# Index products of two heads side by side, with the first pair of a chunk issued inside the logits

## The chip, the cores and the metric

The kernel runs on one core of one Trainium2 chip. The core has five engines that run on their own and meet at semaphores: TensorE (PE, with PEld for its weight loads), VectorE (DVE), ScalarE (ACT), GpSimd (POOL) and SyncE (SP, which here only issues DMAs). The metric is the device time of one execution in microseconds (us).

## What is computed

One decoder layer over 2048 tokens of width 1024, in float32: layer norm, one projection, a pooling mixer and an attention over selected keys, the output projection, a second norm, and a mixture of 32 experts of which each token uses four. The change lies in the attention. There an indexer with 8 heads of width 64 scores every key for every query, and the 256 best keys are kept:

```python
s = jnp.einsum('bqhd,bsd->bqhs', iqb, ikf)                       # 8 index heads, width 64
idx_score = jnp.einsum('bqhs,bqh->bqs', jax.nn.relu(s), iwb * w_scale)
idx_score = jnp.where(causal, idx_score, NEG_INF)
_, sel = lax.top_k(idx_score, 256)
logits = jnp.einsum('bqgrd,bqkgd->bqgrk', qg, k_sel) * (HEAD_DIM ** -0.5)
```

## The kernel before

The program has stages one behind the other: projection (up to about 574 us), attention (574 to about 2290 us), a short placement of tokens to experts, the experts (to about 5100 us), and the combination. The attention stage (`attend_stage`) goes over 16 blocks of 128 queries. Block b sees 128(b+1) keys, `keys[b]`. The keys are cut into chunks of `BANK` = 512, one PSUM bank; the last chunk can be 128, 256 or 384 wide. Blocks 0 and 1 need no selection, so there are scores for blocks 2 to 15 only, 38 chunks in all, 28 of them 512 wide.

The order of the work is written out by hand in `walk`, which every engine runs through with functions of its own. For each of the 6 attention heads of block b it calls `logits(b, i)` (PE writes the four-bank PSUM tile `qk`, the product with `kT` and then the mask, bank by bank), then a part of the search for block b+1, and a "fill" for PE: heads 0 to 5 are followed by the output projection of block b-1, `score(b+2, 0)`, `score(b+2, 1)`, `values(b, 0)`, `score(b+2, 2)` and `score(b+2, 3)`; a `score` whose chunk does not exist falls away. `values(b, 1)` closes the block.

For each head DVE takes the maximum of `qk` (`logits` on DVE, L756 and L759), and ACT then takes the exponential (`exp`, L998), which frees `qk` for the next head: PE waits for it (`s_exp`) before the next logits. In a `score` or `values` fill, ACT takes the head's exponential three quarters of the way through, that is before the seventh of the eight relus.

DVE searches the 256th best score of block b+1 by 32 steps of a bisection over the whole row of keys (`search`, L725 to L730), spread over the six heads by `parts`, a plan that counts PE's columns; then `select` (L737 to L751) writes the mask. PE's first logits of the next block wait for the mask (`s_mask`).

One chunk of `score` on PE: for each of 8 index heads one product with 64 rows, of `iq` and `ikT`, into the two-bank PSUM tile `pair` (L855), ACT's relu of it into `relu` (L983, two buffers), and one product with 128 rows that adds it, times the head's weight, into `acc` (L860). Even heads lie in rows 0 to 63 of `iq` and `ikT`, odd heads in rows 64 to 127. The order on PE is index 0, 1, 2, sum 0, index 3, sum 1, and so on. All are float32 products, and each is two MATMUL instructions in the trace. `claim(*PAIR)` and `claim(*ACC)` make PE wait until what last used `pair` or `acc` has been read out.

SP loads the constants at the start of the stage; every engine but PE waits until all have landed (`s_const`, `CONSTS`), and PE's first logits of block 0 depend on `q` alone.

Of the kernel before, what the change touches and what calls it, by code (L numbers as in the profile page):

```python
# [27 lines left out]
P = 128  # L28
SEQ = 2048
D = 1024  # L30
TILES = SEQ // P
KD = D // P
POOL_W, POOL_GROUPS = D // 4, 4
# [6 lines left out]
IDX_H, IDX_D = 8, 64  # L40
# [16 lines left out]
BANK = 512  # L57
# [320 lines left out]
def attend_stage(nc, A, S, D_):  # L378
# [6 lines left out]
    CLEARS = 16 * 2  # L385
    CONSTS = 16 * 13
    keys = [P * (b + 1) for b in range(TILES)]
# [75 lines left out]
    with ExitStack() as ctx:  # L463
# [10 lines left out]
        bias = sb("bias_1", [P, D])  # L474
        band = sb("band_sb", [P, 3, POOL_GROUPS, P])
        w_pool = sb("w_pool_sb", [P, 2, P])
# [3 lines left out]
        h = sb("h_blk", [P, D])  # L480
        scores = [sb("scores_even", [P, SEQ - P]), sb("scores_odd", [P, SEQ])]
        mask = sb("mask", [P, 2, SEQ], BF16)
        relu = sb("relu", [P, 2, BANK])
        w_diag = sb("w_diag", [P, IDX_H, P])
# [88 lines left out]
        with nc.Block() as block:  # L573
            @block.sync
            def _(sp):
# [6 lines left out]
                def load_q(b):  # L582
# [6 lines left out]
                             allow_slow_non_contiguous=True).then_inc(s_const, 16)  # L589
                sp.dma_start(band[:], A["band"]).then_inc(s_const, 16)  # L590
                sp.wait_ge(s_made, 2)
# [237 lines left out]
            def _(pe):  # L829
# [11 lines left out]
                ACC = ("sc", "diff", "pools", "best", "rk")  # L841

                def score(b, c, head):
                    claim(*PAIR)
                    claim(*ACC)
                    if c == 0:
                        pe.wait_ge(s_iq[b % 2], 16 * ((b - 2) // 2 + 1))
                        pe.wait_ge(s_wd, b - 1)
                    u0 = IDX_H * (chunk0[b] + c)
                    at, width = c * BANK, min(BANK, keys[b] - c * BANK)  # L850
                    for i in range(IDX_H + 2):
                        if i < IDX_H:
                            row = slice(IDX_D * (i % 2), IDX_D * (i % 2 + 1))
                            wait(pe, s_relu, u0 + i - 1)
                            nc.tensor.matmul(pair[:, (u0 + i) % 2, 0:width], iq[row, b % 2, i // 2],  # L855
                                             S["ikT"][row, at:at + width], start=True, stop=True).then_inc(s_idx, 1)
                        if i >= 2:
                            j = i - 2
                            pe.wait_ge(s_relu, u0 + j + 1)
                            nc.tensor.matmul(acc[:, 0:width], w_diag[:, j], relu[:, (u0 + j) % 2, 0:width],  # L860
                                             start=(j == 0), stop=(j == IDX_H - 1)).then_inc(s_wsum, 1)
                    used["relu"] = u0 + IDX_H
                    used["sc"] = chunk0[b] + c + 1

                def logits(b, i):
                    n = HEADS * b + i
                    wait(pe, s_exp, n)
                    if i == 0:
                        pe.wait_ge(s_q[b % 2], 16 * (b // 2 + 1))
                        if b < 2:  # L870
                            pe.wait_ge(s_made, 4)
                        else:
                            pe.wait_ge(s_mask, b - 1)
                    for c in range(-(-keys[b] // BANK)):
                        at, width = c * BANK, min(BANK, keys[b] - c * BANK)
                        nc.tensor.matmul(qk[:, at:at + width], q[:, b % 2, i], S["kT"][:, i // REP, at:at + width],  # L876
                                         start=True, stop=False)
                        op = nc.tensor.matmul(qk[:, at:at + width], ident_bf[:], mask[:, b % 2, at:at + width],  # L878
                                              start=False, stop=True)
                    op.then_inc(s_qk, 1)  # L880

# [26 lines left out]
                def differ(b):  # L908
                    claim(*ACC)
                    if b == 0:  # L910
                        pe.wait_ge(s_const, CONSTS)
                    for g in range(POOL_GROUPS):
                        out = acc[POOL_G * (g % 2):POOL_G * (g % 2 + 1), (g // 2) * P:(g // 2 + 1) * P]
                        cols = slice(g * POOL_G, (g + 1) * POOL_G)
                        op = nc.tensor.matmul(out, S["u"][:, b, cols], band[:, 0 if b == 0 else 1, g],
                                              start=True, stop=(b == 0))
                        if b:
                            op = nc.tensor.matmul(out, S["u"][:, b - 1, cols], band[:, 2, g], start=False, stop=True)
                    op.then_inc(s_diff, 1)
# [54 lines left out]
            def _(act):  # L974
                def score(b, c, head):
                    u0 = IDX_H * (chunk0[b] + c)
                    at, width = c * BANK, min(BANK, keys[b] - c * BANK)
                    for i in range(IDX_H):
                        if i == IDX_H * 3 // 4 and head:
                            exp(*head)  # L980
                        act.wait_ge(s_idx, u0 + i + 1)
                        wait(act, s_wsum, u0 + i - 1)
                        nc.scalar.activation(relu[:, (u0 + i) % 2, 0:width], pair[:, (u0 + i) % 2, 0:width],  # L983
                                             ACT.Relu).then_inc(s_relu, 1)
# [861 lines left out]
```

## Time and profile before

| | us |
|---|---|
| median of 3 runs | 5346.77 (5340.24 to 5354.88) |
| the profiled execution | 5348.82 |
| its span, first to last instruction | 5347.2 |
| PE busy | 4898.8 (92%) |
| DVE busy | 3068.7 (57%) |
| ACT busy | 1842.8 (34%) |
| POOL busy | 980.4 (18%) |

The profile's page groups instructions by line, engine and tile; a group's idle time says what ended the waiting before it. The timeline lists instructions in order of time, neighbours merged: "1.13 ... x4" are four instructions that lasted 1.13 us together. A recorded PE duration contains the way through the array, so neighbouring matmuls overlap in the records, and the distance between their starts is the better measure. PEclk is the granted clock of TensorE: 1.00 is 2.4 GHz, 0.5 is 1.2 GHz.

### The profile page before, as it was taken

To read this page: it belongs to the slowest core of one execution; us is meant where nothing else is said; L and a number is where in the kernel's file an instruction comes from. 1 tells how busy PE (TensorE), PEld (TensorE's weight loads), DVE (VectorE), ACT (ScalarE), POOL (GpSimd) and SP (SyncE) were. 2 spreads that over 40 slices of the span, in tenths; PEclk is the share of its full clock that TensorE was granted. 3 is DMA by queue.
4 is the path that set the end of the run, shared out by engine and by line. 5 is a ranking of instruction groups with operands and counts; after the bars stand their busy time and mean duration, and the time that the engine had idled before them with its cause. 6 is when DMAs were issued, how large, how long until landed. Compare 5 with 4: busy or idle time off the path is not lost. (4 is left out here: it accounts for less than half of the span.)

```text
span 5347.2 us, 68611 instructions
## 1 busy us (share of the span) xinstructions
PE 4898.8 (92%) x23758; PEld 3552.4 (66%) x23759; DVE 3068.7 (57%) x4877; ACT 1842.8 (34%) x2663; POOL 980.4 (18%) x1073
## 2 busy tenths in 40 slices
PE   7999688899999995849999999999999999999977
PEld 3444333344444443448999999999999999999822
DVE  2222167778777778155555655565576556755522
ACT  1111123233333332224343444343454444543400
POOL 0000122111111111121211121121122112211155
PEclk9999789999999997869999999999999999999988
DMA  4332210101000000045454554465565455654355
GB/s 181 114 114 106 78 26 17 22 17 22 13 13 13 12 11 8 8 156 190 165 201 152 204 191 169 146 216 169 183 222 186 169 196 183 223 188 165 133 197 185
DMA packets 426731, 663.73 MB, mean 124 GB/s; under 512 B 22064, under 2 KB 286256, under 8 KB 425552
## 3 DMA queue, kind: packets, MB, share of 16 engines
q1 hardware_dynamic: 367776, 507.46, 29.1%
q0 software_dynamic: 26576, 85.56, 4.5%
q10 hardware_dynamic: 32256, 69.22, 3.4%
q8 instruction: 60, 0.98, 0.1%
q14 instruction: 63, 0.52, 0.0%
HBM read 542.86 MB, written 119.31 MB: 124 GB/s over the span
## 5 line engine op out<-in xcount | busy, mean ns | idle before, releaser
L1352 PE MATMUL gu<-x_hi,w_hi 128*128 128x256 f32 (+2 forms) x4096 | 1230.8, 300 | 1.3 <-DVE x_lo L1434 1.3
L1353 PE MATMUL gu<-x_lo,w_hi 128*128 128x256 f32 (+2 forms) x4096 | 1231.2, 301 | 0.0
L1354 PE MATMUL gu<-x_hi,w_lo 128*128 128x256 f32 (+2 forms) x4096 | 1229.0, 300 | 0.0
L1429 DVE TENSOR_TENSOR w_lo<-w_raw,w_hi 128x2048 fp32r<-128x2048 f32 x386 | 874.4, 2286 | 532.7 <-ACT w_hi L1503 532.7
L1503 ACT ACTIVATE w_hi<-w_raw 128x2048 fp32r<-128x2048 f32 x386 | 727.0, 1907 | 283.0 <-PE gu L1354 196.0
L1352 PEld LDWEIGHTS gu<-x_hi,w_hi 128*128 128x128 f32 x4096 | 772.1, 189 | 2.5 <-issue 1.7
L1354 PEld LDWEIGHTS gu<-x_hi,w_lo 128*128 128x128 f32 x4096 | 772.6, 189 | 0.0
L1353 PEld LDWEIGHTS gu<-x_lo,w_hi 128*128 128x128 f32 x4096 | 770.2, 188 | 0.7
L1325 POOL TENSOR_TENSOR a_lo<-up,a_hi 128x384 fp32r<-128x384 f32 x256 | 396.9, 1550 | 1489.4 <-ACT a_hi L1515 1489.4
L1352 PE MATMUL yp<-w_hi,a_hi 128*128 128x512 f32 x1296 | 526.0, 406 | 0.0
L1353 PE MATMUL yp<-w_lo,a_hi 128*128 128x512 f32 x1296 | 514.8, 397 | 0.0
L1354 PE MATMUL yp<-w_hi,a_lo 128*128 128x512 f32 x1296 | 514.6, 397 | 0.0
L298 PE MATMUL proj_acc<-w_in_sb,hT 128*128 128x512 f32 (+1 forms) x1280 | 474.0, 531 | 7.3 <-DMA w_in_sb<-w_in 5.3
L298 PEld LDWEIGHTS proj_acc<-w_in_sb,hT 128*128 128x128 f32 x1280 | 225.3, 191 | 256.0 <-issue 249.1
L1440 DVE TENSOR_SCALAR gate<-gu,b_gu 128x384 f32<-128x384 f32 x256 | 157.2, 614 | 371.1 <-PE gu L1354 371.1
L725 DVE TENSOR_SCALAR_CACHE_REDUCE mask<-scores_odd,small 128x512 bf16<-128x512 f32 (+6 forms) x224 | 345.9, 1544 | 18.7 <-issue 1.6
L725 DVE TENSOR_SCALAR_CACHE_REDUCE mask<-scores_even,small 128x384 bf16<-128x384 f32 (+6 forms) x224 | 316.1, 1411 | 18.2 <-issue 0.7
L756 DVE TENSOR_REDUCE small<-qk 128x1 f32<-128x128 f32 (+15 forms) x96 | 123.9, 1291 | 324.9 <-PE qk L878 286.9
L876 PE MATMUL qk<-kT,q_blk 128*128 128x512 f32 (+3 forms) x480 | 235.8, 575 | 80.1 <-ACT probs L998 58.6
L860 PE MATMUL acc<-relu,w_diag 128*128 128x512 f32 (+3 forms) x608 | 303.4, 598 | 1.8 <-ACT relu L983 1.6
L855 PE MATMUL pair<-ikT,iq_blk 64*128 64x512 f32 (+3 forms) x608 | 276.4, 600 | 25.1 <-ACT relu L983 23.7
L983 ACT ACTIVATE relu<-pair 128x512 f32<-128x512 f32 (+3 forms) x304 | 161.0, 543 | 396.1 <-PE acc L860 286.6
(256 smaller groups left out, 5898.9 us busy)
## 6 DMA issues: line engine op xcount, KB each, us to landing
w_raw<-w_gate_up SPq DMA_DIRECT2D x258, 1024.0 KB, 7.6
w_raw<-w_down SPq DMA_DIRECT2D x128, 1024.0 KB, 6.4
y_dram<-y_rows ACTq DMA_DIRECT2D x192, 256.0 KB, 3.1
y_dram<-zeros SPq DMA_DIRECT2D x16, 2016.0 KB
h_blk<-h_dram SPq DMA_DIRECT2D x32, 512.0 KB, 6.1
qi_dram<-qi_stage ACTq DMA_DIRECT2D x16, 640.0 KB, 2.9
w_in_sb<-w_in SPq DMA_DIRECT2D x1, 8480.0 KB, 23.9
x_in<-x SPq DMA_DIRECT2D x16, 512.0 KB, 9.2
```

Of the source, the lines that this page charges most:

```text
L298: mm = nc.tensor.matmul(acc[:, n, 0:width], hT[:, slot, k], w_in[:, k, c0:c0 + width], start=(k == 0), stop=(k == KD - 1))
L725: nc.vector.tensor_scalar(reach, s, limit, 0.0, ALU.is_ge, ALU.add, accum_out=n_reach)
L855: nc.tensor.matmul(pair[:, (u0 + i) % 2, 0:width], iq[row, b % 2, i // 2], S["ikT"][row, at:at + width], start=True, stop=True).then_inc(s ...
L860: nc.tensor.matmul(acc[:, 0:width], w_diag[:, j], relu[:, (u0 + j) % 2, 0:width], start=(j == 0), stop=(j == IDX_H - 1)).then_inc(s_wsum, 1)
L876: nc.tensor.matmul(qk[:, at:at + width], q[:, b % 2, i], S["kT"][:, i // REP, at:at + width], start=True, stop=False)
L983: nc.scalar.activation(relu[:, (u0 + i) % 2, 0:width], pair[:, (u0 + i) % 2, 0:width], ACT.Relu).then_inc(s_relu, 1)
L1325: nc.gpsimd.tensor_tensor(a_lo[:, j], up[:, j % 2], a_hi[:, j].bitcast(F32), ALU.subtract).then_inc(s_al, 1)
L1352: nc.tensor.matmul(out, s_hi_, m_hi, start=(n == 0), stop=False)
L1353: nc.tensor.matmul(out, s_hi_, m_lo, start=False, stop=False)
L1354: op = nc.tensor.matmul(out, s_lo_, m_hi, start=False, stop=(n == len(pairs) - 1))
L1429: nc.vector.tensor_tensor(w_lo[:, c % 2, cols], raw[:, c % 3, cols], w_hi[:, c % 2, cols].bitcast(F32), ALU.subtract).then_inc(s_lo, 1)
L1503: nc.scalar.activation(w_hi[:, c % 2, cols], raw[:, c % 3, cols], ACT.Copy).then_inc(s_hi, 1)
```

## The change

Four things.

1. On PE the index products are issued in pairs, rows 0 to 63 and 64 to 127 directly behind each other with one wait ahead of both, into the two banks of `pair`. The order becomes pair, two sums, pair, two sums, pair, four sums.
2. The first pair of a chunk moves forward into the logits ahead of it: it stands behind the first bank of `logits(b, i)`, with the claim of `pair` ahead of it.
3. `relu` has three buffers in place of two, and ACT's wait for a free buffer looks one further back. ACT's own order stays, with the exponential before the seventh relu.
4. To make room, `band` (weights of the pooling mixer) keeps two of its three parts, and the part that only block 0 uses is loaded into `scores_odd`. That is one DMA more among the constants.

```diff
-    CONSTS = 16 * 13
+    CONSTS = 16 * 14
...
-        band = sb("band_sb", [P, 3, POOL_GROUPS, P])
+        band = sb("band_sb", [P, 2, POOL_GROUPS, P])
...
+        band0 = scores[1][:, 0:POOL_GROUPS * P].rearrange("p (g n) -> p g n", n=P)
         mask = sb("mask", [P, 2, SEQ], BF16)
-        relu = sb("relu", [P, 2, BANK])
+        relu = sb("relu", [P, 3, BANK])
...
-                sp.dma_start(band[:], A["band"]).then_inc(s_const, 16)
+                sp.dma_start(band[:], A["band"][:, 1:3]).then_inc(s_const, 16)
+                sp.dma_start(band0, A["band"][:, 0]).then_inc(s_const, 16)
...
+                def index(b, c, i):
+
+                    u = IDX_H * (chunk0[b] + c) + i
+                    at, width = c * BANK, min(BANK, keys[b] - c * BANK)
+                    if i:
+                        pe.wait_ge(s_relu, u)
+                    for j in range(2):
+                        rows = slice(IDX_D * j, IDX_D * (j + 1))
+                        nc.tensor.matmul(pair[:, j, 0:width], iq[rows, b % 2, i // 2],
+                                         S["ikT"][rows, at:at + width], start=True, stop=True).then_inc(s_idx, 1)
+
+                def begin_score(b, c):
+                    claim(*PAIR)
+                    if c == 0:
+                        pe.wait_ge(s_iq[b % 2], 16 * ((b - 2) // 2 + 1))
+                    index(b, c, 0)
+
                 def score(b, c, head):
-                    claim(*PAIR)
                     claim(*ACC)
                     if c == 0:
-                        pe.wait_ge(s_iq[b % 2], 16 * ((b - 2) // 2 + 1))
                         pe.wait_ge(s_wd, b - 1)
                     u0 = IDX_H * (chunk0[b] + c)
-                    at, width = c * BANK, min(BANK, keys[b] - c * BANK)
-                    for i in range(IDX_H + 2):
-                        if i < IDX_H:
-                            row = slice(IDX_D * (i % 2), IDX_D * (i % 2 + 1))
-                            wait(pe, s_relu, u0 + i - 1)
-                            nc.tensor.matmul(pair[:, (u0 + i) % 2, 0:width], iq[row, b % 2, i // 2],
-                                             S["ikT"][row, at:at + width], start=True, stop=True).then_inc(s_idx, 1)
-                        if i >= 2:
-                            j = i - 2
-                            pe.wait_ge(s_relu, u0 + j + 1)
-                            nc.tensor.matmul(acc[:, 0:width], w_diag[:, j], relu[:, (u0 + j) % 2, 0:width],
+                    width = min(BANK, keys[b] - c * BANK)
+                    for i in range(0, IDX_H, 2):
+                        if i + 2 < IDX_H:
+                            index(b, c, i + 2)
+                        else:
+                            pe.wait_ge(s_relu, u0 + IDX_H)
+                        for j in (i, i + 1):
+                            nc.tensor.matmul(acc[:, 0:width], w_diag[:, j], relu[:, (u0 + j) % 3, 0:width],
...
+                    chunk = {1: 0, 2: 1, 4: 2, 5: 3}.get(i)
                     for c in range(-(-keys[b] // BANK)):
...
                         op = nc.tensor.matmul(qk[:, at:at + width], ident_bf[:], mask[:, b % 2, at:at + width],
                                               start=False, stop=True)
+                        if c == 0 and chunk is not None and b + 2 < TILES and chunk < chunks[b + 2]:
+                            begin_score(b + 2, chunk)
...
-                        wait(act, s_wsum, u0 + i - 1)
-                        nc.scalar.activation(relu[:, (u0 + i) % 2, 0:width], pair[:, (u0 + i) % 2, 0:width],
+                        wait(act, s_wsum, u0 + i - 2)
+                        nc.scalar.activation(relu[:, (u0 + i) % 3, 0:width], pair[:, i % 2, 0:width],
```

The order on PE before, in block 11: the end of the logits of head 1 (L876 and L878, three banks) and the first chunk of scores for block 13. Behind L855 the waits for what used `pair` and `acc` are listed by the names of their semaphores.

```order
L876 MATMUL qk<-kT,q_blk 128x512
L878 MATMUL qk<-mask,ident_bf 128x512
L855 MATMUL pair<-ikT,iq_blk 128x512 [waits a_pools,a_best,a_sc,a_rks,a_ov,a_iq1,a_hts,a_wd,a_res,a_relu,a_pts]
L855 MATMUL pair<-ikT,iq_blk 128x512 [waits a_relu] x2
L860 MATMUL acc<-relu,w_diag 128x512 [waits a_relu]
L855 MATMUL pair<-ikT,iq_blk 128x512 [waits a_relu]
L860 MATMUL acc<-relu,w_diag 128x512 [waits a_relu]
```

In this listing the index products and the sums then alternate to the end, where three sums stand together. The same place on PE in the changed kernel, from the logits' first bank on (L893 and L895 are the logits now, L854 the index products, L875 the sums):

```order
L893 MATMUL qk<-kT,q_blk 128x512 [waits a_exp]
L895 MATMUL qk<-mask,ident_bf 128x512
L854 MATMUL pair<-ikT,iq_blk 128x512 [waits a_hts,a_ov,a_res,a_iq1,a_pts,a_relu]
L854 MATMUL pair<-ikT,iq_blk 128x512
L893 MATMUL qk<-kT,q_blk 128x512
L895 MATMUL qk<-mask,ident_bf 128x512
...
L854 MATMUL pair<-ikT,iq_blk 128x512 [waits a_rks,a_wd,a_best,a_relu,a_pools,a_sc]
L854 MATMUL pair<-ikT,iq_blk 128x512
L875 MATMUL acc<-relu,w_diag 128x512 x2
L854 MATMUL pair<-ikT,iq_blk 128x512 [waits a_relu]
L854 MATMUL pair<-ikT,iq_blk 128x512
```

The first two index products and the wait for `pair` moved ahead of the second bank of the logits, and each later pair stands ahead of two sums.

## Rows read from the trace of the kernel before

**Rows 1.** Busy time by block (blocks 7, 11, 13, 14), columns named in the first row.

```profile
core 0: us, PE busy (x) PEld busy (x) DVE busy (x) ACT busy (x) POOL busy (x), PEclk, DMA share, GB/s
...
1133.00:1234.00 101.00, 95.14 (x303) 43.03 (x303) 80.95 (x170) 34.78 (x70) 17.25 (x27) 0.98 0.09 18
...
1579.00:1711.00 132.00, 122.77 (x391) 54.19 (x390) 104.02 (x170) 46.17 (x86) 23.66 (x27) 1.00 0.04 14
...
1851.00:1994.00 143.00, 137.22 (x429) 60.79 (x428) 114.01 (x170) 50.66 (x89) 17.54 (x19) 0.99 0.04 11
1994.00:2139.00 145.00, 86.46 (x313) 47.05 (x313) 120.05 (x170) 33.45 (x58) 16.13 (x19) 0.80 0.02 8
```

**Rows 2.** Timeline, block 11: logits of head 1, then scores, chunk 0.

```profile
1598.10 1.02 PE L876 MATMUL qk<-kT,q_blk 128*128 128x512 f32 x2
...
1598.30 1.02 ACT L1039 ACTIVATE res<-pair 128x1024 f32<-128x1024 f32 x1 [11.79 <-PE pair L938]
...
1598.96 0.38 PE L878 MATMUL qk<-mask,ident_bf 128*128 128x512 bf16 x1
...
1601.11 0.38 PE L878 MATMUL qk<-mask,ident_bf 128*128 128x512 bf16 x1
...
1601.41 1.13 PE L855 MATMUL pair<-ikT,iq_blk 64*128 64x512 f32 x4
...
1602.58 1.08 ACT L983 ACTIVATE relu<-pair 128x512 f32<-128x512 f32 x2 [3.25 <-PE pair L855]
...
1603.22 1.12 PE L855 MATMUL pair<-ikT,iq_blk 64*128 64x512 f32 x2 [0.68 <-ACT relu L983]
...
1604.28 1.13 PE L860 MATMUL acc<-relu,w_diag 128*128 128x512 f32 x2
...
1605.33 1.12 PE L855 MATMUL pair<-ikT,iq_blk 64*128 64x512 f32 x2
1605.50 0.60 ACT L983 ACTIVATE relu<-pair 128x512 f32<-128x512 f32 x1 [1.84 <-PE acc L860]
```

**Rows 3.** Timeline of PE, block 11: chunk 0's end, then the `values` loop.

```profile
1614.82 3.00 PE L860 MATMUL acc<-relu,w_diag 128*128 128x512 f32 x6
...
1643.65 0.49 PE L893 MATMUL pair<-ident,probs 128*128 128x128 f32 x3
1643.98 0.81 PE L898 MATMUL o_acc<-probsT,v_sb 128*128 128x384 f32 x2
1644.63 0.49 PE L893 MATMUL pair<-ident,probs 128*128 128x128 f32 x3
```

**Rows 4.** Waits of DVE in blocks 1 to 5: total us, times, longest.

```profile
DVE small L756 <- PE qk L878: 58.7, 16, 12.0
```

**Rows 5.** The same in blocks 6 to 8.

```profile
DVE small L756 <- PE qk L878: 26.7, 9, 4.6
```

**Rows 6.** The same in blocks 9 to 13.

```profile
DVE small L756 <- PE qk L878: 87.5, 19, 9.9
```

**Rows 7.** The same in block 11 alone.

```profile
DVE small L756 <- PE qk L878: 17.7, 3, 7.8
```

**Rows 8.** Timeline of DVE, opening waits of blocks 1, 5 and 9.

```profile
642.67 0.42 DVE L756 TENSOR_REDUCE small<-qk 128x1 f32<-128x256 f32 x1 [5.36 <-PE qk L878]
...
950.39 0.96 DVE L756 TENSOR_REDUCE small<-qk 128x1 f32<-128x768 f32 x1 [8.56 <-PE qk L878]
...
1343.28 1.49 DVE L756 TENSOR_REDUCE small<-qk 128x1 f32<-128x1280 f32 x1 [4.27 <-PE qk L878]
```

**Rows 9.** Timeline of ACT in block 11, chunk 0: the head's exponential.

```profile
1612.32 1.53 ACT L998 ACTIVATE probs<-qk,small 128x1536 f32<-128x1536 f32 x1
```

**Rows 10.** Windows with PE's clock, before and after a wait of PE.

```profile
1435.40:1438.80 3.40, 3.40 (x22) 1.00 0.01 0
1442.20:1445.60 3.40, 3.15 (x8) 0.51 0.95 93
```

**Rows 11.** Timeline of PE between these two windows.

```profile
1441.40 0.88 PE L893 MATMUL pair<-ident,probs 128*128 128x128 f32 x6 [2.15 <-ACT probs L998]
```

**Rows 12.** Timeline at the stage's start: SP's issues, DVE's first wait.

```profile
571.29 0.47 SPq L590 DMA_DIRECT2D band_sb<-band  x1
...
573.33 0.35 SPq L592 DMA_DIRECT2D lists_dram<-res  x1
...
599.57 0.29 DVE L756 TENSOR_REDUCE small<-qk 128x1 f32<-128x128 f32 x1 [35.48 <-DMA w_out_sb<-w_out]
```

More of the change, by code:

```diff
@@ L914, in differ @@
                         cols = slice(g * POOL_G, (g + 1) * POOL_G)
-                        op = nc.tensor.matmul(out, S["u"][:, b, cols], band[:, 0 if b == 0 else 1, g],
+                        op = nc.tensor.matmul(out, S["u"][:, b, cols], band[:, 0, g] if b else band0[:, g],
                                               start=True, stop=(b == 0))
                         if b:
-                            op = nc.tensor.matmul(out, S["u"][:, b - 1, cols], band[:, 2, g], start=False, stop=True)
+                            op = nc.tensor.matmul(out, S["u"][:, b - 1, cols], band[:, 1, g], start=False, stop=True)
                     op.then_inc(s_diff, 1)
```

## The prediction

> **What bounds the kernel now.** I read the busy time by block first. In blocks 7 to 13 PE is busy 93 to 96% of the block at nearly full clock, so PE sets the pace there. But DVE is close behind: 114 of 143 us in block 13, and its drains between dependent small instructions are not counted as busy [rows 1]. In block 14, where there are no scores left to make, DVE's 120 us of work make the block as long as the one before although PE is busy for 86 only [rows 1]: DVE is the next bound, and it is near. How near is what DVE waits for PE: 58.7 us in blocks 1 to 5, 26.7 in 6 to 8, 87.5 in 9 to 13 [rows 4 to 6]. Then I read one chunk instruction by instruction [rows 2, 3]. Everything outside the attention is untouched and only starts earlier.
>
> **A chunk on PE, before.** A float32 product of 512 columns takes 0.86 us (L876 to L878, both 128 rows) [rows 2]. In the score loop the step from an index product to a sum, or back, takes 1.05 us [rows 2], so each change between 64 and 128 rows costs 0.20 us. It is not the semaphore wait that costs it: in the `values` loop a wait stands ahead of each step too, and three transposes and a product follow each other in 0.33 and 0.65 us, their bare columns [rows 3]. From 1601.41 to the end of the last sum at about 1617.65 a full chunk takes 16.2 us. It holds 7 index steps, not 8: the four instructions of heads 0 and 1 lasted 1.13 us together, as long as the two of one head (1.12) [rows 2]. **The side-by-side running is thus already in the trace**, once per chunk. After it PE idles 0.68 us for the first relu [rows 2].
>
> **After.** Three pairs and eight sums stand in the score: 11 steps of 0.86 and 6 changes of rows of 0.20, 10.6 us. The pair inside the logits adds one step and two changes, 1.3 us. Together 11.9, against 16.2: **4.3 us less per full chunk.** Of that 2.6 are the three index steps (scaling with the width), the rest changes of rows and the idle time. A chunk of 384, 256, 128 columns then saves about 3.5, 2.7, 1.7.
>
> Do the relus keep up? Relu 3 needs a free buffer, that is sum 0. From the start of a sum to the relu that waited for it is 1.22 us, and the relu takes 0.60 [rows 2], so the next pair may start 1.86 us after sum 0 did; PE's own order brings it there after 1.9. That fits with nothing to spare; I take 0 and keep 0.3 per pair (34 us in all) for the range. Relu 1, which the second pair needs, is hidden behind the remaining banks of the logits from block 8 on; in blocks 1 to 3 the logits have one bank, and some 1.2 us of each chunk's saving goes.
>
> The claim of `pair` inside the logits of head 1 meets ACT's copy of `res` out of `pair`: it ran 1598.30 to 1599.32, and the logits' first bank ends at 1599.17 [rows 2], so PE waits about 0.2 us. At the other heads the last reader of `pair` is older. Logits end 1.3 us later after they begin, which holds up DVE only where it waits anyway.
>
> The added DMA is one issue of 0.47 us on SP, but SP then waited until 573.33 for POOL [rows 12]; that wait hides it. If not, it is 0.5 us, since w_out's landing starts DVE. Bytes are the same.
>
> **What PE could save.** Blocks 1 to 5, 6 to 8 and 9 to 13 make 6, 6 and 16 full chunks and one of each narrow width per group: 33.7, 33.7 and 76.7 us. Block 0 makes one of 384 columns at half clock, about 4. Sum 148.
>
> **What DVE lets through.** A block cannot be shorter than DVE's own work, so the saving is at most the waiting of DVE that PE can take away.
> - Blocks 9 to 13: 87.5, less what must stay at each opening. DVE writes the mask, then PE needs all of head 0's logits, 1.07 us per bank, some 0.3 more until DVE starts: 3 to 4 us for five blocks, 17.5 in all (block 9's opening wait of 4.27 is nearly all of this kind [rows 8]). That leaves 70, below PE's 76.7.
> - Blocks 6 to 8: 26.7 less 7.5 is 19.
> - Blocks 1 to 5: the five opening waits, 5.36 the first and 8.56 the last [rows 8], add up to 38.2 and come from the block's tail, which has no scores in it. 20.5 is left.
> - Block 0: DVE is idle, 4.
>
> The ceiling is 70 + 19 + 20.5 + 4 = 114. It is not reached, since the waits lie at certain heads. Block 11 has three: 7.8 at the opening and 9.9 shared by heads 2 and 5 [rows 7]. Chunk 0 gives 4.3, which the wait before head 2 can take. Chunk 1 gives 4.3 where there is no wait, so DVE falls behind by it. Chunk 2 gives 4.3, which meets the wait before head 5; chunk 3 meets the opening, where 4 are usable. About 12.5 of PE's 15.6 arrive. And falling behind costs something new: ACT takes the exponential before relu 6 and before the change reached it 10.9 us after the logits' end (1612.32) [rows 2, 9]; now it gets there after 5.9, while DVE's maximum, late by 4.3 plus its own 1.8 and what it was late before, is ready at 6 to 8. PE then stands 0 to 2 us before its last sums. I take 5 of 6 parts of the ceiling in blocks 9 to 13 (58), two thirds in 6 to 8 (13), and 12 and 4 in the rest: **87 us**.
>
> **What the new idle time costs.** Where DVE is late, PE waits at the block's end for the mask. After a wait of 2.15 us [rows 11] the granted clock was 0.51 in the next 3.4 us, against 1.00 before it [rows 10], so PE was at 1.2 in place of 2.4 GHz. If that falls on the opening logits, for which DVE waits, it costs up to 1.7 us a block. For 13 blocks that is 0 to 22; I take 9, and 3 for the 14 claims at 0.2. **87 - 12 = 75 us.**
>
> The Trainium skill, TensorE: Matmul & The Clock Gate, section "Why this matters for your kernels", advises to leave PE no idle gaps between bursts of matmuls, since it falls back to half rate. By that rule a change that frees PE while DVE stays the bound hands part of its gain back; the rows on the clock agree.
>
> **Rivals.**
> - *PE's gain arrives nearly whole* (105 to 148 less, 5199 to 5242). For it: DVE's lateness is made good wherever a wait follows. Against it: block 14, where DVE alone sets 145 us [rows 1]. 12%.
> - *DVE takes most of it* (20 to 50 less, 5297 to 5327): lateness piles up over heads 3 and 4, and each exponential holds back the relus. Only the waits before head 2 and at the openings are used. The two rows of `pair` not running side by side belongs here too: 16 steps with 8 changes are 15.4 us, 0.8 less than before, 30 us in all. Against that is the x4 row [rows 2]. Together 16%.
> - *Gain and idle cost cancel*: within 16 us. 7%.
> - *Slower.* The pair inside the logits delays the maximum by 1.3 us at 38 heads. Where DVE is the bound and stands waiting for exactly these logits, this is 49 us on its path; with the clock at 1.2 GHz during them up to twice that, 98. It decides once DVE is early at these heads but late at the block's end, so that the score's saving is worth nothing. Against it: DVE comes to three heads of block 11 without any wait [rows 7]. With 40 of PE's gain still arriving the time is 5347 + 98 - 40 = 5405. 4%.
> - *The clock rule in full*: every new wait of PE is followed by 3.4 us at half clock in all 38 chunks, 1.7 us each, 65 us off the 87, so 22 less, 5325. Against it: PE now waits 0.68 us in each of these chunks [rows 2] and the clock is 1.00 through block 11 [rows 1]. 4%.
>
> **How the numbers follow.** Forecast 57%, with 50 to 105 less; the rivals 12, 16, 7, 4 and 4. The profiled execution took 5348.8 (span 5347.2), 2.0 above the median of 5346.8; 75 less gives 5273.8 and 5271.8, and I state 5272. The range leaves out the tails: 5224 below (a little beyond DVE's ceiling), 5322 above (34 us for the relus and the full clock cost). Faster by over 0.3% (16 us, about what a measurement of this kernel tells from no change) 0.89, within it 0.07, slower 0.04.
>
> **What would show it.** Right: the index products in pairs with equal starts, pairs to sums 1.05 us apart; a full chunk from its second pair on in 10.6 us; DVE's waits in blocks 9 to 13 down from 87.5 to some 25, and new waits of PE for the exponential and for the mask; block 14 unchanged near 145. Wrong: index starts 0.86 apart (not side by side); a wait of PE for relus in each pair; DVE's waits unchanged with the block as long as before; or a time outside the attention that moves.

## The result, and the profile of the changed kernel

| | before | changed |
|---|---|---|
| median of 4 runs, us | 5344.09 (5340.24 to 5354.88) | 5249.94 (5243.35 to 5252.06) |
| the profiled execution | 5348.82 | 5250.43 |
| attention, first logits to the placement | 1720.1 | 1621.0 |
| experts, first to last product | 2720.6 | 2720.7 |
| from there to the end | 275.1 | 275.5 |

The ratio is 0.9819, 95% interval 0.9801 to 0.9836: about 97 us less, at 75 forecast. All of it lies in the attention. The same blocks as in [rows 1], in windows of the changed kernel:

```profile
core 0: us, PE busy (x) PEld busy (x) DVE busy (x) ACT busy (x) POOL busy (x), PEclk, DMA share, GB/s
1096.00:1192.00 96.00, 87.30 (x296) 42.12 (x300) 80.89 (x170) 34.36 (x69) 17.49 (x27) 0.95 0.08 19
1518.00:1639.00 121.00, 112.84 (x387) 54.10 (x393) 102.81 (x170) 46.11 (x86) 19.65 (x27) 0.97 0.04 15
1763.00:1896.00 133.00, 124.58 (x423) 58.42 (x428) 114.20 (x171) 51.06 (x90) 18.02 (x20) 0.97 0.04 12
1896.00:2041.00 145.00, 86.57 (x308) 47.81 (x312) 120.21 (x171) 32.47 (x56) 15.87 (x18) 0.80 0.02 8
```

DVE's work is what it was (114.20 against 114.01 us in block 13), PE has 12.6 us less there, and the block is 10 us shorter. Block 14, which makes no scores, is as long as before. DVE's waits for the logits in blocks 1 to 5, 6 to 8 and 9 to 13, the same as in [rows 4 to 6] and with the columns as there:

```profile
DVE small L759 <- PE qk L895: 24.7, 9, 5.4
DVE small L759 <- remote: 12.2, 1, 12.2
...
DVE small L759 <- PE qk L895: 15.6, 8, 4.4
...
DVE small L759 <- PE qk L895: 36.7, 13, 6.3
```

The row "remote" is block 3's opening wait under another name (12.0 before). The gain is what these waits fell by: a block's length less these waits is DVE's own time, and that hardly changed (338.7 us before and 337.1 now in blocks 1 to 5, 275.0 and 275.2 in 6 to 8, 566.6 and 563.6 in 9 to 13). From first logits to first logits:

| blocks | before | changed | gain | DVE's waits fell by | predicted gain |
|---|---|---|---|---|---|
| 0 | 66.9 | 56.5 | 10.4 | | 4 |
| 1 to 5 | 397.4 | 374.0 | 23.4 | 21.8 | 12 |
| 6 to 8 | 301.6 | 290.7 | 10.9 | 11.1 | 13 |
| 9 to 13 | 654.1 | 600.3 | 53.8 | 50.8 | 58 |
| 14 | 144.3 | 144.4 | -0.1 | | 0 |

PE in block 11 of the changed kernel: the end of head 1's logits, then the whole score of a full chunk. Compare [rows 2, 3].

```profile
1538.12 0.38 PE L895 MATMUL qk<-mask,ident_bf 128*128 128x512 bf16 x1
1538.69 1.13 PE L854 MATMUL pair<-ikT,iq_blk 64*128 64x512 f32 x4 [0.19 <-issue]
1539.75 2.20 PE L893 MATMUL qk<-kT,q_blk 128*128 128x512 f32 x4
...
1542.10 1.13 PE L854 MATMUL pair<-ikT,iq_blk 64*128 64x512 f32 x4
1543.15 1.99 PE L875 MATMUL acc<-relu,w_diag 128*128 128x512 f32 x4
1545.07 1.13 PE L854 MATMUL pair<-ikT,iq_blk 64*128 64x512 f32 x4
1546.13 1.98 PE L875 MATMUL acc<-relu,w_diag 128*128 128x512 f32 x4
1548.04 1.13 PE L854 MATMUL pair<-ikT,iq_blk 64*128 64x512 f32 x4
1549.10 3.86 PE L875 MATMUL acc<-relu,w_diag 128*128 128x512 f32 x8
```

Every pair lasts 1.13 us, and its sums start 1.05 or 1.06 us behind it. The last sum ends at 1549.10 + 3.86 = 1552.96 by the record; read with the same 0.17 us off as in the prediction (1614.82 + 3.00 became 1617.65), that is 1552.8, or 10.7 us from the second pair on. No pair of this chunk waits for a relu. The first pair stands inside the logits, with 0.19 us of claim ahead. ACT beside it:

```profile
1544.38 0.60 ACT L1002 ACTIVATE relu<-pair 128x512 f32<-128x512 f32 x1 [0.53 <-PE acc L875]
...
1547.84 1.54 ACT L1017 ACTIVATE probs<-qk,small 128x1536 f32<-128x1536 f32 x1
```

The exponential starts 5.7 us after the logits' end (1542.10). What PE waits for in blocks 1 to 13 is new (before, the rows were `r_diag` 35.2 us, relus 23.2, `probsT` 18.9, `probs` 6.7):

```profile
PE o_acc L917 <- ACT probsT L1029: 36.6, 33, 4.9
PE pair L923 <- POOL r_diag L676: 21.5, 10, 9.5
PE acc L943 <- ACT oT L1041: 14.5, 3, 5.9
PE pair L912 <- ACT probs L1017: 14.4, 5, 6.7
PE pair L854 <- ACT relu L1002: 9.2, 17, 1.2
PE acc L875 <- ACT relu L1002: 7.2, 6, 3.1
```

PE's idle time in these blocks rose from 114.8 to 141.8 us: it waits for ACT's exponentials and their transposes, and the exponentials wait for DVE's maximum (132.9 us of ACT's idle time, 40 times).

### The profile page after: what moved, and what is told of

The parts are those of the page before. It is cut to its first block and busy times, and to the rows that moved or that the text cites. A ratio compares the mean times of both kernels' runs of the same rounds, so it can differ in the third digit from the quotient of the medians.

```text
span 5248.9 us, 68534 instructions
## 1 busy us (share of the span) xinstructions
PE 4773.0 (91%) x23705; PEld 3529.8 (67%) x23759; DVE 3065.1 (58%) x4877; ACT 1841.8 (35%) x2663; POOL 977.8 (19%) x1073
## 5 line engine op out<-in xcount | busy, mean ns | idle before, releaser
L893 PE MATMUL qk<-kT,q_blk 128*128 128x512 f32 (+3 forms) x480 | 238.1, 580 | 92.5 <-ACT probs L1017 62.0
L917 PE MATMUL o_acc<-probsT,v_sb 128*128 128x384 f32 x544 | 249.7, 549 | 40.6 <-ACT probsT L1029 40.6
L1373 PEld LDWEIGHTS yp<-w_hi,a_lo 128*128 128x128 f32 x1296 | 245.0, 189 | 59.5
L1371 PEld LDWEIGHTS yp<-w_hi,a_hi 128*128 128x128 f32 x1296 | 245.4, 189 | 55.3
L1372 PEld LDWEIGHTS yp<-w_lo,a_hi 128*128 128x128 f32 x1296 | 245.7, 190 | 52.8
```

The costliest lines, as they stand in the source:

```text
L917: nc.tensor.matmul(o_acc[:].rearrange("p a b -> p (a b)"), S["v"][:, c - 1, g * HEAD:(g + 1) * HEAD], probsT[:, (v0 + c - 1) % 2].rearrang ...
L1371: nc.tensor.matmul(out, s_hi_, m_hi, start=(n == 0), stop=False)
L1372: nc.tensor.matmul(out, s_hi_, m_lo, start=False, stop=False)
L1373: op = nc.tensor.matmul(out, s_lo_, m_hi, start=False, stop=(n == len(pairs) - 1))
```

## The experiments

Each ratio is to the kernel before on the same chip. Its median was 5361.17 us on the chip of experiments 1 to 4, 5353.44 on the chip of the repetition in experiment 2 and of experiment 5, and 5354.48 on the chip of experiments 6 to 9. The attention trace of one kernel differs by some 10 us between chips (the changed kernel: 1621.0 and 1630.2), so ratios decide and traces explain.

**1. Are the pairs side by side, and is that what pays?** Both products of a pair use rows 0 to 63, in the order and with the waits of the changed kernel. This leaves out the odd index heads; the work is as much.

```diff
-                        rows = slice(IDX_D * j, IDX_D * (j + 1))
+                        rows = slice(0, IDX_D)
```

> The changed kernel, but both products of a pair take rows 0 to 63, so the second one repeats the first head instead of computing its own (odd index heads are left out; the mask and the routing behind it can differ, so the attention stage is read from the trace by itself). Theory: the gain comes from two products running side by side. Then a pair costs two steps of 0.86 us in place of one, four more steps or 3.4 us per full chunk on PE; of the 98 us that the attention gained 60 to 75 go away again, some 5315 us in all, and the four instructions of a pair last about 2.0 us. Rival: the gain comes from the fewer changes between 64 and 128 rows and from the relu wait; then the time stays within 15 us of 5250.

Measured 5335.71 us, ratio 0.9945 (0.9928 to 0.9961). PE, block 11:

```profile
1605.99 1.98 PE L854 MATMUL pair<-ikT,iq_blk 64*128 64x512 f32 x4
1607.90 1.99 PE L875 MATMUL acc<-relu,w_diag 128*128 128x512 f32 x4
```

A pair takes 1.98 us in place of 1.13. Some 64 to 67 of the 97 us are gone with nothing else changed: running in the two halves of the rows carries two thirds of the gain. Order, buffers and the moved pair without it leave 29 us by the ratio (21 to 39), and 9 by the traces of the attention (1710.7 us against 1720.1). 29 is close to the 30 that the prediction gave to the rival "not side by side". The parts do not simply add up: experiment 9 loses about half of the gain with the pairs still side by side.

**2. Pairs alone.** `begin_score` moves out of the logits to the start of `score`.

```diff
                 def score(b, c, head):
+                    begin_score(b, c)
                     claim(*ACC)
...
-                        if c == 0 and chunk is not None and b + 2 < TILES and chunk < chunks[b + 2]:
-                            begin_score(b + 2, chunk)
```

> The changed kernel, but the first pair of a chunk is issued at the start of the scores and not inside the logits. Per full chunk one change of rows less (0.2 us less), and PE waits for relu 1, about 1.3 us more: some 1.0 to 1.2 us more per chunk, 35 us on PE. Theory (DVE is the bound now): half of it is absorbed, about 5268 us, and DVE waits more before the heads that follow the scores. Rival (PE is still the bound): 35 us more, 5285.

Measured 5258.94 us, 0.9807 (0.9791 to 0.9824): as good as the changed kernel, which had run on another chip. So both ran again on one chip.

> The changed kernel once more, on the same chip as the next three. Expected: the same ratio to the kernel before as in the result, 0.982.

> The changed kernel without the early pair (the first pair stands at the start of the scores), beside the changed kernel on one chip. On another chip its ratio to the kernel before was 0.981, no worse than the changed kernel's 0.982. Theory: since DVE sets the blocks, PE's 1 us per chunk for the early pair is worth 5 to 12 us. Rival: it is worth nothing, within 4 us.

Measured 5257.80 us, 0.9825 (0.9806 to 0.9844) for the changed kernel, and 5257.91, 0.9822 (0.9801 to 0.9843) for pairs alone. The medians are 0.1 us apart, and the four runs of each spread over 5 and 11 us: the theory's 5 to 12 us did not show, and the moved pair is worth nothing here that these runs could tell. PE, block 11, pairs alone:

```profile
1547.05 1.13 PE L854 MATMUL pair<-ikT,iq_blk 64*128 64x512 f32 x4
1549.44 1.13 PE L854 MATMUL pair<-ikT,iq_blk 64*128 64x512 f32 x4 [1.26 <-ACT relu L1001]
```

The wait that the move hides is there, up to 1.3 us per chunk, and PE is idle for 166.5 and 162.2 us in blocks 1 to 13 (two traces) where it was 141.8 and 151.5. The attention is no longer for it (1631.6 and 1628.7 us against 1621.0 and 1630.2). So more idle time of PE costs nothing here. The move also ends each logits 1.3 us later, for which DVE may be waiting; how much the one gives and the other takes was not separated.

**3. The early products alone**, on the kernel before: index products 0 and 1 go into the logits, each with its wait, the rest stays in the old order.

```diff
+                def begin_score(b, c):
+                    claim(*PAIR)
...
+                    index(b, c, 0)
+                    index(b, c, 1)
...
-                        if i < IDX_H:
...
+                        if 2 <= i < IDX_H:
+                            index(b, c, i)
```

> The kernel before, with only the first two index products of each chunk moved into the logits, behind the first bank; the order after it stays index, sum, index, sum, with two relu buffers. Theory: it takes away the 0.68 us wait for the first relu and adds two changes of rows (0.4 us), 0.3 us less per chunk, about 10 us in all, 5335 us. Rival: the early pair carries a good part of the gain by itself, 5310 or less.

Measured 5339.59 us, 0.9956 (0.9939 to 0.9972): 24 us less, 15 to 33, between theory and rival. There PE sets the pace, and the move hides the 0.68 us before index product 2 [rows 2] in 38 chunks, 26 us at most. The trace of that run shows only 7 us less attention than the trace of before, which is within what two chips differ. That the same move is worth something on the kernel before, and nothing that showed behind the pairs, is measured; its exact size is not.

**4. Is DVE late because the plan of its search is out of date?** `parts` still counts columns as the old score had them. Here the shares follow durations read from the trace.

```diff
-        work = [(KD + 1) * D, 2 * IDX_H * width[0], 2 * IDX_H * width[1], (s + 1) * group,
-                2 * IDX_H * width[2] + D, 2 * IDX_H * width[3] + D + (s + 1) * group]
...
+        work = [15.5, chunk[0], chunk[1], values, chunk[2] + 3.4, chunk[3] + 1.0 + values]
```

> The changed kernel with another plan for the search: the bits are shared out by the times that the traces show (a chunk of scores 11.9 us, the projection 15.5, and so on, and DVE's other work of each head taken off first) and no longer by PE's columns; the same bits in all, 1 to 3 of them moved from heads 2 and 3 to head 4. Theory: DVE comes 4 to 7 us late to head 3 and that holds PE in the values loop, so a better share gives 8 to 25 us, about 5235. Rival: DVE's total work alone sets the block, then it stays within 5 us of 5250.

Measured 5254.13 us, 0.9796 (0.9780 to 0.9812), beside 0.9807 for pairs alone on the same chip and 0.9819 and 0.9825 for the changed kernel on others: not told apart, though a gain of some 10 us is not excluded. The plan did what it was meant to: DVE's lateness at head 3 fell from 7.1 to 2.7 us in block 6 and from 6.5 to 3.9 in block 11. But its waits in blocks 9 to 13 stayed:

```profile
DVE small L762 <- PE qk L898: 38.1, 15, 7.3
```

and so did the blocks (124.0 and 127.3, 133.1 and 135.2 us in blocks 12 and 13). Of these waits 25.2 us are the five opening waits, which no share of the search can fill, since the next part of the search stands behind the first maximum. The theory (8 to 25 us) did not show; moving DVE's work within a block was worth nothing that could be told.

**5. Is DVE's total the bound now, and was it not before?** The bisection takes 28 steps in place of 32, so the last four bits of the threshold are left out; once in the changed kernel, once in the one before.

```diff
-    BITS, SELECT = 32, 5
+    BITS, SELECT = 28, 5
```

> The changed kernel with 28 in place of 32 steps of the search (the last four bits of the threshold are left out, so the selection is only approximately the same). It takes about 115 us of work from DVE in blocks 1 to 14 together, 12 of them in block 14. Theory (DVE sets blocks 1 to 13 now): 45 to 60 us less than the changed kernel, since PE's saving of 148 us then arrives nearly whole. Rival (PE is still the bound): only block 14 gets shorter, 12 to 20 us less.

> The kernel before with the same four steps of the search left out. Theory: PE was the bound in blocks 1 to 13, so only block 14 and a little elsewhere get shorter, 12 to 25 us less than the kernel before. Rival (DVE was a bound before too): 45 us less or more.

Measured 5203.39 us, 0.9725 (0.9706 to 0.9743) in the changed kernel, 54 us below it; and 5347.96 us, 0.9991 (0.9980 to 1.0001), 5 us and hardly told from nothing, in the one before. DVE's own time in blocks 1 to 14 (their length less its waits for the logits) fell by 111 us in the changed kernel. Of that 51 arrived and 60 became new waits, so DVE bounds the blocks now, but PE is close behind: half of what DVE saves arrives. In the kernel before 116 us were saved and 112 became waits. DVE's waits in blocks 9 to 13 of the changed kernel, then of the kernel before from 1345 us on (which leaves out the 4.4 us of block 9's opening):

```profile
DVE small L759 <- PE qk L895: 60.4, 19, 9.8
```

```profile
DVE small L756 <- PE qk L878: 144.7, 23, 18.6
```

In the kernel before I had expected 12 to 25 us, mostly from block 14, and that block did lose 13. But blocks 10 to 12 grew by 6.8, 6.9 and 2.5 us, together 16. Without that growth, which the changed kernel does not have, the four steps would be worth some 20 us there (an estimate, 5 and 16), so 54 against 5 overstates what relieving PE did. POOL tells why; first with 28 steps, then with 32, block 11:

```profile
1692.23 8.55 POOL L657 TENSOR_SCALAR w_diag<-ident,iw_sb 128x128 f32<-128x128 f32 x8
1700.96 2.84 POOL L697 DMA_INDIRECT lists_dram<-token,at_i  x1 [0.18 <-issue]
...
1713.87 1.07 POOL L673 TENSOR_SCALAR r_diag<-ident,small 128x128 f32<-128x128 f32 x3 [6.27 <-DMA lists_dram<-token,at_i]
```

```profile
1692.72 2.81 POOL L657 TENSOR_SCALAR w_diag<-ident,iw_sb 128x128 f32<-128x128 f32 x8
...
1709.46 1.07 POOL L673 TENSOR_SCALAR r_diag<-ident,small 128x128 f32<-128x128 f32 x3 [2.49 <-DMA lists_dram<-token,at_i]
```

DVE came to `select` earlier, and in these 8.55 us it ran (28 steps):

```profile
1691.25 1.92 DVE L737 TENSOR_SCALAR_CACHE_REDUCE mask<-scores_even,small 128x1664 bf16<-128x1664 f32 x1
...
1693.26 2.12 DVE L739 SCALAR_TENSOR_TENSOR scores_even<-scores_even,small,mask 128x1664 f32<-128x1664 f32 x1
...
1695.52 1.03 DVE L742 TENSOR_SCALAR mask<-scores_even 128x1664 bf16<-128x1664 f32 x1
...
1696.87 3.74 DVE L747 TENSOR_TENSOR_SCAN mask<-mask 128x1664 bf16<-128x1664 bf16 x1
```

Taken one by one, POOL's eight instructions last 0.37 us each but for three: the one beside L739 lasts 2.00 us, the one beside L742 1.19 and the one beside L747 3.67, each ending 0.2 us after that DVE instruction. Three ran beside L737 at 0.37, and those that began just before or together with L739 and L747 took 0.37 too. Blocks 10 and 12 show the same three (1.87, 1.12, 3.40 and 2.13, 1.25, 3.93 us). POOL lost 5.74 us in block 11. Its scatter, then `r_diag`, came late, and PE stood up to 8.7 us for it where it had been 3.8. The Trainium skill, SBUF — State Buffer, section "Who interferes with whom", says that a DVE instruction with two inputs in SBUF contends with a GpSimd instruction that reads SBUF; L739 and L747 have two such inputs, L737 has one, and the trace agrees. L742 has one too and stretched POOL all the same, which this sentence does not cover. In the changed kernel with 28 steps no instruction of POOL's eight is stretched in any block (369 ns in the mean).

**6. Take `r_diag` out from behind the scatter.** The `r_diag` wait is PE's second largest in the changed kernel. On POOL the scatter of tokens stands ahead of it; here it stands behind `values(b, 1)`.

```diff
-            piece("scatter", b - 2)
             piece("inverse", b, 1)
...
             piece("values", b, 1, None)
+            piece("scatter", b - 2)
```

> The changed kernel with one move in the order by hand: the scatter of a block (POOL's four indirect DMAs and the wait for them) stands behind the second values step instead of ahead of it, so that POOL writes r_diag, for which PE waits at the end of a block, without the scatter in front. In the changed kernel PE waited for r_diag 10 times, 21.5 us in blocks 1 to 13. Theory: these waits are at the block's end, where DVE waits for PE as well (opening waits of 5 to 6 us in blocks 9 to 13, of which 3 to 4 must stay), so 8 to 15 us less than the changed kernel, ratio 0.980. Rival: DVE hides it, less than 4 us.

Measured 5236.83 us, 0.9775 (0.9759 to 0.9791), the fastest kernel here that does the whole computation. Its interval lies below both of the changed kernel's (0.9819 and 0.9825). How far below is less sure: 24 to 27 us by the ratios across chips, but 15 on its own chip, where the kernel of experiment 8 took 5247.78 us (one run), some 3.6 less than the changed kernel would, and 11 to 20 by the attention's traces (1610.1 us against 1621.0 and 1630.2). At the end of block 2, POOL and then PE of the changed kernel:

```profile
763.80 1.07 POOL L676 TENSOR_SCALAR r_diag<-ident,small 128x128 f32<-128x128 f32 x3 [9.70 <-DMA lists_dram<-token,at_i]
```

```profile
764.93 1.65 PE L923 MATMUL pair<-r_diag,ones 128*128 128x384 f32 x2 [9.46 <-POOL r_diag L676]
```

and POOL with the scatter late, then PE's waits over blocks 1 to 13 of that kernel (from 641 us on):

```profile
750.70 1.63 POOL L676 TENSOR_SCALAR r_diag<-ident,small 128x128 f32<-128x128 f32 x3 [2.90 <-DVE small L774]
```

```profile
PE qk L893 <- DVE mask L754: 14.9, 5, 5.4
...
PE pair L923 <- POOL r_diag L676: 3.3, 2, 2.2
```

Block 2 fell from 74.5 to 64.8 us, and block 3's opening wait of DVE from 12.2 to 1.5. In blocks 9 to 13, where I had placed the gain, the lengths stayed (600.5 against 600.3 us): the `r_diag` waits there (5.4 us) went, and waits for the mask, that is for DVE, rose from 1.6 to 14.0. The size was as expected (8 to 15 us) if the comparison on its own chip holds, and above it by the ratios; the place was not.

**7. The exponential later**, on top of 6: in the first `values` of a block ACT takes the exponential of head 3 just ahead of its last copy, and no longer three quarters of the way through.

```diff
-                        if c == b * 3 // 4 and head:
+                        if c == b and head:
```

> The last kernel, and in the values step ACT takes the exponential of the head before the last copy and not three quarters of the way through. In the changed kernel PE waited 36.6 us for ACT's copies there, since ACT stood at an exponential whose maximum DVE had not yet written. Theory (DVE sets the blocks): PE's waiting there mostly turns into waiting elsewhere, 0 to 8 us less than the last kernel. Rival: PE's 36.6 us are on the path, 15 us less or more.

Measured 5239.07 us, 0.9783 (0.9767 to 0.9799): no difference from 6. PE's wait for `probsT` fell from 37.1 to 31.1 us and that of the sums for relus rose from 7.7 to 15.1.

**8. What does the clock cost?** In blocks 8 and 9 of the changed kernel PE waits for head 5's exponential ahead of `values(b, 1)`, at the block's end, and the clock falls. Here 5 and 7 products that nobody reads fill that wait.

```diff
-                    pe.wait_ge(s_exp, HEADS * b + REP * (g + 1))
                     claim(*PAIR)
+                    for _ in range({8: 5, 9: 7}.get(b, 0) if g else 0):
+                        nc.tensor.matmul(pair[:, 0], S["ident"][:], S["kT"][:, 0, 0:BANK], start=True, stop=True)
+                    pe.wait_ge(s_exp, HEADS * b + REP * (g + 1))
```

> The changed kernel with 5 and 7 products added on PE in blocks 8 and 9, in the places where PE waited 4.6 and 6.7 us for the exponential ahead of the second values step; nothing reads them. After these waits TensorE's granted clock was 0.5 for 6.8 and 10.2 us. Theory: PE stays at full clock there, and 2 to 3 us of each drop were on the path; block 8 takes 101 to 102 us (103.0 in two traces), block 9 104 to 105 (106.7 in two). Rival: DVE's lateness hides the clock, both blocks stay within 0.5 us.

One run, 5247.78 us. Block 9 of the changed kernel: PE behind the wait, then two windows, ahead of it and over the `values` that follow (columns as in the first windows above):

```profile
1388.95 1.54 PE L912 MATMUL pair<-ident,probs 128*128 128x128 f32 x6 [6.74 <-ACT probs L1017]
```

```profile
1377.00:1382.00 5.00, 4.95 (x32) 3.67 (x31) 4.52 (x9) 1.57 (x4) 4.23 (x7) 1.00 0.01 0
1384.10:1394.30 10.20, 5.35 (x16) 3.58 (x17) 9.41 (x16) 2.89 (x5) 2.31 (x2) 0.53 0.51 109
```

and with the products:

```profile
1379.41 6.25 PE L905 MATMUL pair<-kT,ident 128*128 128x512 f32 x14
```

```profile
1386.00:1396.00 10.00, 9.43 (x48) 6.22 (x48) 9.33 (x13) 5.02 (x12) 2.37 (x3) 1.00 0.21 77
```

The clock stayed at 1.00 (2.4 GHz) instead of 0.53, and six transposes took 0.88 us instead of 1.54. Blocks 8 and 9 took 101.5 and 104.6 us against 103.0 and 106.7 (the same two numbers in both traces of the changed kernel): the clock costs some 1.5 and 2.1 us of the path in these two places. The sizes are rough, since pairs alone, with no products added, took 101.9 and 102.5 us in block 8 in its two traces, though 107.4 and 107.7 in block 9.

**9. Is the third relu buffer needed?** The changed kernel with two.

```diff
-        relu = sb("relu", [P, 3, BANK])
+        relu = sb("relu", [P, 2, BANK])
...
-                        wait(act, s_wsum, u0 + i - 2)
+                        wait(act, s_wsum, u0 + i - 1)
```

> The changed kernel with two relu buffers in place of three. Relu 3 then waits for sum 1 and not sum 0, and the next pair for relu 3: 0.85 us more before each of the second and third pair of a chunk's scores, and the last sums wait too, 2 to 2.5 us more per full chunk on PE, 75 us over all chunks. Theory: DVE absorbs about half, 30 to 45 us above the changed kernel, ratio 0.989. Rival: the third buffer is not needed, within 5 us.

Measured 5303.27 us, 0.9895 (0.9879 to 0.9912): 38 to 41 us above the changed kernel by the ratios, about 52 on the same chip, reckoned as in experiment 6. The pairs behind a chunk's first now wait; one of them in block 11, then the total from 641 to 1890 us:

```profile
1603.79 1.13 PE L854 MATMUL pair<-ikT,iq_blk 64*128 64x512 f32 x4 [0.75 <-ACT relu L1002]
```

```profile
PE pair L854 <- ACT relu L1002: 57.2, 81, 1.2
```

The buffer is worth two fifths to half of the whole gain.

## Why the prediction was right, and where its sizes were off

**Pairs run side by side: right.** Pair to sum 1.05 us; the chunk from its second pair 10.7 us at 10.6 predicted. Experiment 1 shows the cause: 1.98 us in the same rows, 1.13 in two halves, and two thirds of the gain with it.

**No wait for relus in each pair: right**, and the margin was as thin as worked out: the relu ends at 1544.38 + 0.60, and the next pair starts 0.09 us later. The `pair` waits are 9.2 us in all; experiment 9 shows 0.75 us per pair without the third buffer.

**DVE sets the ceiling: right.** Group by group the gain is what DVE's waits fell by (21.8 of 23.4, 11.1 of 10.9, 50.8 of 53.8 us), block 14 did not move, and four search steps less are worth 54 us in the changed kernel (experiment 5). It is a ceiling with PE close under it, since only half of what DVE saved there arrived. New waits of PE for exponential and mask came as said, those for the mask small (2.8 us in blocks 1 to 13). DVE's waits in blocks 9 to 13 fell to 36.7 us, not to 25, so a little less arrived: 53.8 at 58. The term that was too small is what must stay at the openings: I took 3 to 4 us each, 17.5 in all, and the five measured 5.0 to 6.3, 27.8 in all. The waits at the other heads went almost entirely, from 52.8 to 8.9 us.

**Block 0: mis-sized**, 10.4 us at 4. I took the narrow chunk at half clock before and after. Two windows, of before and of the changed kernel, with the clock third from the end:

```profile
602.00:625.00 23.00, 22.43 (x33) 7.98 (x34) 0.45 (x2) 4.17 (x10) 0.00 (x0) 0.50 0.05 11
```

```profile
602.00:617.00 15.00, 13.27 (x38) 5.77 (x38) 0.60 (x3) 5.04 (x13) 0.00 (x0) 0.74 0.06 17
```

A mean of 0.74 over 15 us is 7.2 us at full clock: the clock rose to full at 609.8 us in place of 626.5, and stayed there for 10 us. A change of work also moves the moment at which the clock rises. No run was made for its cause, but the traces narrow it: the clock rose at 614.2 us with both products in the same rows (experiment 1), at 611.1 with pairs alone (2) and at 610.3 with two relu buffers (9), and only at 626.9 with the early products in the old order (3). So it is neither the running side by side nor the moved pair nor the third buffer that it needs; the order in pairs is what is left, with the moved load of `band`, and the two were not separated.

**Blocks 1 to 5: mis-sized**, 23.4 us at 12. The step that failed is that the opening waits come from a tail that the scores do not reach. The openings of blocks 4 and 5 fell from 11.1 to 2.9 and from 8.6 to 2.2 us, while the waits at the other heads gave 7.6 of the 12 that I had taken from them. DVE had come to these openings early, and PE late, because of the scores ahead; with less of these, PE reached the tail sooner. Experiments 1 and 9, which take much of PE's saving back, bear this out: block 4's opening is 12.1 and 11.8 us in them. Of the long ones that of block 3 alone stayed (12.0 and 12.2), and experiment 6 shows its cause: POOL's scatter ahead of `r_diag`, which PE's speed does not touch.

**The 12 us of new idle cost: mechanism right, deduction not seen as a loss of its own.** The mean clock of blocks 1 to 13 fell from 0.96 to 0.95, and the granted clock stood at 0.5 for 129 us in them against 101, with PE busy for 102 and 84 of these. Experiment 8 gives 1.5 and 2.1 us on the path in two places, against up to 1.7 per block in the prediction. But the groups already contain it: they sum to 98 us with nothing left to take off. The claim inside the logits of head 1 in block 11 cost 0.19 us, as said.

**How 75 and 98 go together.** Not each term was right: block 0 gave 6 us more than forecast, blocks 1 to 5 gave 11 more, 6 to 8 2 less and 9 to 13 4 less, and the 12 taken off were not seen. That the time still lies in the range, 50 to 105 us less, is owed to the mechanism, which had the largest group within 4 us, and in part to the width of the range.

**The rival that came closest** is the gain that arrives nearly whole (105 to 148 us); 97 lies between it and the 87 of my own sum. Blocks 9 to 13 and 6 to 8 followed the forecast; the extra is in blocks 0 to 5. None of the slower rivals showed. Experiment 2 is the nearest to the one on delayed logits: taking the pair out of the logits gained nothing, so the delay cost no more than the wait that it hides.

## What to carry to other kernels

Ask of a change that frees one engine how long the next one waits for it, stage by stage: those waits, and not the freed time, are the ceiling of the gain. Here DVE waited 172.9 us in blocks 1 to 13, PE could save some 144, and 88 arrived. How much of a wait must stay is read from its end: for the openings 5 to 6 us each, where I had taken 3 to 4. A second edit that only saves time of the freed engine was then worth nothing that showed (the moved pair, experiment 2), and one that gave the new bound back its time paid about half (28 steps: 111 us of DVE's time, 51 of the attention's), because the freed engine is close behind. And look what stands ahead of a waited-for instruction on a lightly loaded engine: moving POOL's scatter behind it gained 11 to 27 us, by the measure taken, with no work saved.

## What the runs showed of the hardware

POOL's eight small multiplications took 8.55 us instead of 2.81 where DVE ran `select` beside them, so that less work on DVE made blocks longer. Over the kernel before the mean of one was 374 ns with 32 steps and 526 ns with 28:

```profile
L657 POOL TENSOR_SCALAR w_diag<-ident,iw_sb 128x128 f32<-128x128 f32 x112 | 39.4, 374 | 0.1
```

```profile
L657 POOL TENSOR_SCALAR w_diag<-ident,iw_sb 128x128 f32<-128x128 f32 x112 | 56.6, 526 | 0.1
```

Only nine of the 112 make the difference, three in each of blocks 10 to 12. Each ran beside `select`'s L739, L742 or L747 and lasted about as long as that instruction, up to 3.93 us.

And the clock can rise 17 us sooner for a change in what PE runs (block 0). That gave 6 us more than the estimate that left the clock at half; which part of the change does it is narrowed down to the order in pairs or the moved load, and not shown.
